# Early attention scores from split fp32r operands in place of one fp32 product, in a two-layer decoder trunk on one Trainium2 core

## What is computed

```python
DILATED_GROUPS = ((128, 1), (512, 4), (2048, 16))
kv = shared_kv(x, kv_norm, w_kv)
parts = jnp.split(jnp.einsum('bsd,de->bse', h, w_in), N_GROUPS + 1, axis=-1)
s = jnp.einsum('nbqhd,nbkhd->nbhqk', qb, kk) * (HEAD_DIM ** -0.5) + bias
s = jnp.where(mask[None, :, None], s, -jnp.inf)
p = jnp.exp(s - m)
```

## Time and profile before

| | before |
|---|---|
| median of 3 runs | 1452.63 us (1452.29 to 1452.71) |
| the profiled execution | 1452.75 us |
| its span, first to last instruction | 1450.9 us |
| PE busy | 1432.3 us, 99% of the span, 10707 matmul records |
| PEld busy | 1397.7 us, 96% |
| DVE busy | 860.2 us, 59% |
| ACT busy | 686.7 us, 47% |
| POOL busy | 384.9 us, 27% |
| mean granted TensorE clock | 0.999 of full speed |

### The profile page before, as it was taken

One profiled execution on the slowest core, in us unless ns is written; L12 is line 12 of the kernel. 1 busy time (PEld: TensorE's weight loads), 2 busy tenths in 40 slices (PEclk: granted clock), 3 DMA queues, 4 the chain that ended last, 5 costly groups with the idle time before them and its releaser, 6 DMA issues.

```text
span 1450.9 us, 26919 instructions
## 1 busy us (share of the span) xinstructions
PE 1432.3 (99%) x10707; PEld 1397.7 (96%) x10707; DVE 860.2 (59%) x1391; ACT 686.7 (47%) x1055; POOL 384.9 (27%) x169
## 2 busy tenths in 40 slices
PE   7999999999999999999999999999999999999997
PEld 6999999988999999999999999999999999999886
DVE  3899999622556555465664656646566455664633
ACT  6344444675644444344443444434454344543643
POOL 5888888788300000000000000000000000000785
PEclk9999999999999999999999999999999999999999
DMA  9666767556696566666666666666666666665652
GB/s 277 177 195 179 197 182 196 165 189 205 179 277 182 166 184 187 179 181 168 184 183 179 183 170 184 180 177 185 173 184 177 176 189 173 184 175 160 234 195 87
DMA packets 455089, 268.50 MB, mean 185 GB/s; under 512 B 4491, under 2 KB 437211, under 8 KB 454668
## 3 DMA queue, kind: packets, MB, share of 16 engines
q1 hardware_dynamic: 454572, 267.11, 64.6%
q10 hardware_dynamic: 480, 0.90, 0.2%
HBM read 263.70 MB, written 4.29 MB: 185 GB/s over the span
## 4 chain that ended last, share of the span: by engine, by line
PE 98%; ACT 1%; DVE 0%; ACTq 0%; issue 0%
PE bank L417 21%; PE bank L418 21%; PE bank L419 20%; PE bank L393 6%; PE bank L392 6%; PE bank L394 6%; PE bank L437 4%; PE bank L438 4%; PE bank L439 4%; PE bank L1407 1%; PE bank L1422 1%; PE bank L1391 1%; ACT mem_a L642 0%; PE bank L1397 0%; PE bank L1419 0%; PE bank L1418 0%
## 5 line engine op out<-in xcount | busy, mean ns | idle before, releaser
L357 POOL TENSOR_TENSOR w_lo<-raw,w_hi 128x1024 fp32r<-128x1024 f32 x159 | 381.5, 2410 | 1038.5 <-ACT w_hi L348 1038.0
L348 ACT ACTIVATE w_hi<-raw 128x1024 fp32r<-128x1024 f32 x382 | 399.5, 1061 | 493.6 <-PE bank L419 290.3
L417 PE MATMUL bank<-mem_a,w_hi 128*128 128x256 f32 x1536 | 432.3, 281 | 1.5 <-DVE mem_a L928 1.5
L418 PE MATMUL bank<-mem_a,w_hi 128*128 128x256 f32 x1536 | 429.8, 280 | 0.0
L419 PE MATMUL bank<-mem_a,w_lo 128*128 128x256 f32 x1536 | 427.6, 278 | 0.0
L357 DVE TENSOR_TENSOR w_lo<-raw,w_hi 128x1024 fp32r<-128x1024 f32 x224 | 269.9, 1223 | 242.2 <-ACT w_hi L348 242.0
L417 PEld LDWEIGHTS bank<-mem_a,w_hi 128*128 128x128 f32 x1536 | 288.4, 188 | 4.0 <-DVE mem_a L928 1.6
L418 PEld LDWEIGHTS bank<-mem_a,w_hi 128*128 128x128 f32 x1536 | 290.4, 189 | 0.1
L419 PEld LDWEIGHTS bank<-mem_a,w_lo 128*128 128x128 f32 x1536 | 288.5, 188 | 0.0
L417 PE MATMUL bank<-mem_b,w_hi 128*128 128x256 f32 x1024 | 287.7, 281 | 0.0
L418 PE MATMUL bank<-mem_b,w_hi 128*128 128x256 f32 x1024 | 285.8, 279 | 0.0
(11 more groups left out here) (174 smaller groups left out, 1455.6 us busy)
## 6 DMA issues: line engine op xcount, KB each, us to landing
raw<-w_kv_dram SPq DMA_DIRECT2D x96, 1024.0 KB, 6.1
raw<-b_w_in_dram SPq DMA_DIRECT2D x64, 1024.0 KB, 7.2
raw<-a_w_in_dram SPq DMA_DIRECT2D x47, 1024.0 KB, 5.8
raw<-a_w_out_dram SPq DMA_DIRECT2D x16, 1024.0 KB, 5.1
raw<-b_w_out_dram SPq DMA_DIRECT2D x16, 1024.0 KB, 5.2
bias<-bias_dram SPq DMA_DIRECT2D x16, 384.0 KB, 6.5
x_sb<-x_dram SPq DMA_DIRECT2D x4, 512.0 KB, 5.6
resid_dram<-x_sb SPq DMA_DIRECT2D x1, 2048.0 KB, 10.5
```

Of the source, the lines that this page charges most:

```text
L348: nc.scalar.activation(w_hi[:, stream.half_slot(half), :], raw[:, slot, part:part + HALF], ACT.Copy).then_inc(hi_done, 1)
L357: eng.tensor_tensor(w_lo[:, stream.half_slot(half), :], raw[:, slot, part:part + HALF], w_hi[:, stream.half_slot(half), :].bitcast(F32), A ...
L417: nc.tensor.matmul(dst[:, 0:S], wide_hi, source(kt, 0), start=(kt == 0), stop=False)
L418: nc.tensor.matmul(dst[:, 0:S], wide_hi, source(kt, 1), start=False, stop=False)
```

## The change

The early half of the queries is split as the late half is. `q_hi` and `q_lo` hold all 256 queries of a group and `q_t` is gone; ACT makes `q_hi` with one copy of 256 columns in place of two of 128; DVE's `q_lo` is 256 columns wide in place of 128 and waits for `q_his`; the semaphore `q_copied` is gone. PE makes each early product as three fp32r matmuls of 128 moving columns. `r_row` and `rk_row` move to the place that `taps` has, declared just ahead of it. What is declared behind the queries in SBUF shifts by a few hundred bytes.

```diff
+        r_row, rk_row = shared(("r_row", [P, S], F32), ("rk_row", [P, S], F32))
         taps = sb("taps", [P, TAPS, KT])
...
-        q_t = sb("q_t", [P, NG, P])
-        q_hi, q_lo = sb("q_hi", [P, NG, P], F32R), sb("q_lo", [P, NG, P], F32R)
+        q_hi, q_lo = sb("q_hi", [P, NG, S], F32R), sb("q_lo", [P, NG, S], F32R)
...
-        r_row = sb("r_row", [P, S])
-        rk_row = sb("rk_row", [P, S])
...
-                nc.scalar.activation(q_hi[:, j - NG, :], bank[j % 2][:, P:S], ACT.Copy).then_inc(q_his, 1)
-                nc.scalar.activation(q_t[:, j - NG, :], bank[j % 2][:, 0:P], ACT.Copy).then_inc(q_copied, 1)
+                nc.scalar.activation(q_hi[:, j - NG, :], bank[j % 2][:, 0:S], ACT.Copy).then_inc(q_his, 1)
...
-                dve.wait_ge(q_copied, h * NG + g + 1)
-                nc.vector.tensor_tensor(q_lo[:, g, :], bank[(NG + g) % 2][:, P:S], q_hi[:, g, :].bitcast(F32),
+                dve.wait_ge(q_his, h * NG + g + 1)
+                nc.vector.tensor_tensor(q_lo[:, g, :], bank[(NG + g) % 2][:, 0:S], q_hi[:, g, :].bitcast(F32),
...
-                pe.wait_ge(q_copied, (h + 1) * NG)
                 pe.wait_ge(k_split, (h + 1) * NG)
                 pe.wait_ge(q_split, (h + 1) * NG)
                 for g in range(NG):
-                    nc.tensor.matmul(bank[2][:, g * P:(g + 1) * P], q_t[:, g, :], k_t[:, g, P:2 * P],
-                                     start=True, stop=True)
+                    early = bank[2][:, g * P:(g + 1) * P]
+                    nc.tensor.matmul(early, q_hi[:, g, 0:P], k_hi[:, g, P:S], start=True, stop=False)
+                    nc.tensor.matmul(early, q_hi[:, g, 0:P], k_lo[:, g, P:S], start=False, stop=False)
+                    nc.tensor.matmul(early, q_lo[:, g, 0:P], k_hi[:, g, P:S], start=False, stop=True)
                 for g in range(NG):
                     dst = bank[3][:, g * S:(g + 1) * S] if g < 2 else bank[4][:, 0:S]
-                    nc.tensor.matmul(dst, q_hi[:, g, :], k_hi[:, g, :], start=True, stop=False)
-                    nc.tensor.matmul(dst, q_hi[:, g, :], k_lo[:, g, :], start=False, stop=False)
-                    mm = nc.tensor.matmul(dst, q_lo[:, g, :], k_hi[:, g, :], start=False, stop=True)
+                    nc.tensor.matmul(dst, q_hi[:, g, P:S], k_hi[:, g, :], start=True, stop=False)
+                    nc.tensor.matmul(dst, q_hi[:, g, P:S], k_lo[:, g, :], start=False, stop=False)
+                    mm = nc.tensor.matmul(dst, q_lo[:, g, P:S], k_hi[:, g, :], start=False, stop=True)
```

More of the change, by code:

```diff
@@ L274, in build @@
         gained = sem("gained")
-        q_copied, kz_copied = sem("q_copied"), sem("kz_copied")
+        kz_copied = sem("kz_copied")
         seeded = sem("seeded")
```

## The result

| | before | changed |
|---|---|---|
| median of 7 runs each, side by side | 1452.6 us (1452.23 to 1452.81) | 1457.88 us (1457.52 to 1457.94) |
| ratio, 95% interval | | 1.0036 (1.0026 to 1.0046) |
| the profiled execution | 1452.75 us | 1457.91 us |
| its span | 1450.9 us | 1456.1 us |

The change makes the kernel slower by 5.3 us, 0.36%. The prediction was 1458.1 us.

What follows compares the result with a forecast made beforehand. PE's work was taken to bound the kernel: nine fp32r products at 0.112 us replace 0.67 us of fp32 per head, +0.34 us, +5.4 over 16 heads, all else nothing, giving 1458.1 us. The range was 1450.0 to 1460.2 us.

Steps and rivals of the forecast that it cites:

- PE alone counts: In the sixteen heads PE waits for nobody, so a nanosecond more of PE work is a nanosecond of kernel time.
- The fp32 products stand at the pace of their loads: Early scores: 0.11 us per record is the pace of loading 128 four-byte weight columns; three products cost 0.67 us per head.
- The narrow fp32r product costs 0.112: Early scores: each 128-column fp32r product takes one weight load's pace, 0.112 us, bounded between 0.059 and 0.119.
- Nine times that is 1.01 us, +0.34 a head: Early scores: nine fp32r matmuls replace three fp32 products of 0.67 us per head; +5.4 us over 16 heads.
- Nothing from ACT, DVE, the softmax or the memory: Wider copies and subtractions, a softmax 0.34 us later and moved rows cost nothing; memory position at most 0.6 us either way.
- the reason given for the banks: q_lo subtractions on DVE start earlier, following the first copy, so the bank is free as early as before; cost nothing.
- load-bound case: Early products paced by weight loads: +5.1 to +6.4 us, 0.6 to either side, 1457.2 to 1460.0 us; 70%.
- streaming alone sets the pace: Rival for the early products: 0.059 us each, -0.14 us per head, 1450.2 to 1450.5 us; 12%.
- The counting by passes: Skill page's objection: three products stream 3 x 128 columns against 4 x 128 for one fp32 product, so the change gains.
- The partial overlap of load and stream: Rival for the early products: pace halfway, 0.085 us, +0.10 us per head, +1.6 us, 1454.3 us; 4%.
- The 81 ns: Skill's figure per load and product pair at 128 columns: +0.06 us per head, some +1 us, 1453.7 us.
- a narrow fp32r product is run as two: Rival for the early products: two records or their time, 0.222 us each, +1.33 us per head, 1474.0 us; 14%.

Runs made afterwards that it cites:

- e10: The changed kernel with its three early fp32r matmuls of a group issued twice, the second set overwriting the first: 1474.4 us, ratio to before 1.015.
- e5: The kernel before, its early fp32 products with 64 stationary columns instead of 128: 1457.29 us, ratio 1.003.
- e9: The kernel before, each late product (256 moving columns) as one fp32 product instead of three fp32r ones, q_lo term left out: 1456.29 us, ratio 1.0025.
- e1: The changed kernel, each early product with 64 moving columns instead of 128: 1457.63 us, ratio to before 1.0035.
- e2: The changed kernel, each early product with 64 stationary columns instead of 128, still 128 moving: 1451.22 us, ratio to before 0.9991.
- e6: The changed kernel, but each early product again one fp32 product of q_hi and k_t, q_lo term left out: 1452.82 us, ratio to before 0.9999.
- e8: The kernel before, layer 1 projections loading w_hi once per tile for one 512-column product, halves added by DVE, r_row and rk_row moved: 1451.07 us, ratio 0.9988.

## Why the prediction was right

**PE alone counts.** Right. PE waits nowhere in the heads before or after, and e10 adds PE work that comes back whole.

**The fp32 products stand at the pace of their loads.** Only half shown. e5 halves the load, and the records stay 0.109 apart, so the load alone does not set this pace: there is a second floor just beside it, which is streaming if e9's pace a column holds at 128, or else a fixed time for an fp32 record. The row with one moving column fits a load's floor and a fixed one alike. For the sum it made no difference, since 0.111 was read off directly.

**The narrow fp32r product costs 0.112.** This was the unknown term, between 0.059 and 0.119, and I took the pace of an fp32 load because the loads were equally long. The value was right, but the reason was weaker than it sounds: the length of a load's record does not give its pace. In the kernel before, the nine fp32 transposes of a head have loads of 141 ns, a quarter shorter, and they stand (1.01 - 0.141) / 8 = 0.109 apart all the same (PEld's group, then its timeline):

```profile
L1407 PEld LDWEIGHTS bank<-ident,prob 128*128 128x128 f32 x144 | 16.1, 141 | 0.1
509.94 1.01 PEld L1407 LDWEIGHTS bank<-ident,prob 128*128 128x128 f32 x9
```

The distance came out at 0.11 by the timeline. e1 and e2 make it a cause rather than a match: the distance follows the stationary columns and not the moving ones.

**Nine times that is 1.01 us, +0.34 a head.** Measured 1.00 and +0.33; 5.4 forecast, 5.3 measured. That the total is so close has some luck in it: the first product costs 0.06 and not 0.112, since its load is hidden, and most of what that saves comes back at the first late product.

**Nothing from ACT, DVE, the softmax or the memory.** Right in the sum; e6 has them alone, 0.04 us from before. The forecasts of total busy time were too large (DVE +6 against +3.6, ACT -7 against -2.9), because they were counts times durations. And the reason given for the banks was not right: the last `q_lo` of head 1 does not start earlier, but at 482.97 against 482.63, which is the 0.34 us that PE is later by then; it ends 0.14 us later beside PE, and the cover of over 11 us takes that. By the prediction's own terms its load-bound case runs from 1457.1 to 1459.6; it wrote 1457.2 to 1460.0, which changes nothing.

**The rivals.** That streaming alone sets the pace is what e2 shows once the load is halved; with 128 stationary columns it doesn't come into play. The counting by passes orders the two forms rightly at 256 columns and fails at 128: in e9 an fp32 product of 256 columns takes 0.432 us, 3.6 times the 0.119 of one fp32r product, and the split form wins. At 128 columns each fp32r product streams for 0.06 and waits for a load of 0.112, three loads in all, while an fp32 product has two records of 0.111. The Trainium skill, "FP8 and Floating Point Precision", section TensorE Precision Notes, gives four passes to true fp32; e9's 3.6 is near that. The partial overlap of load and stream is excluded at this width: a distance of 0.085 appears nowhere, and 0.11 stays when streaming is halved to 0.03 (e1). The 81 ns that "TensorE: Matmul & The Clock Gate", section Back-to-back issue gap, of the Trainium skill gives for 128 columns is met by no run here: 112 ns with 128 stationary four-byte columns, 60 with 64. That a narrow fp32r product is run as two is excluded by the records, one per product.

## What to carry to other kernels

Price a short matmul as the longer of its weight load and its streaming, and count loads: here one load of 128 four-byte columns is 0.112 us, which covers nearly 256 moving columns in fp32r (0.117 to 0.119 apart) or 128 in fp32 (0.109). So splitting one fp32 product into three fp32r ones gains at 256 columns and loses at 128; by these rows (2 x 0.84 ns a column against 3 x 0.112 us) they should be level near 200, which is an estimate, not a run. And where PE streams without a gap, saving loads gains next to nothing (1.8 us in e8): look first which of the two is the longer.

## What I had not expected

- As I read these rows, the record of a matmul is opened when its predecessor has streamed, and stands open while its weights load. 0.22 us is a narrow product that had its weights, 0.27 to 0.28 one that waited for them; the difference, some 0.055, is that between the distances of 0.112 and 0.06. A record's length, so read, tells which of the two bounds the product; the prediction took the 0.36 of the first late product for a start that shows too early.
- fp32 products with 64 stationary columns cost 0.32 us more per block than those with 128 (e5), because loads are not started ahead at the block's two edges (0.25 and 0.17 us idle on PEld). fp32r products with 64 columns have no such gap.
- A 512-column operand in two pieces of 256 takes about 0.23 us (a tile of 0.35 less 0.117), a contiguous one 0.2265; what parts them, the gap in the middle or the alternation with a 256-column product, is open.
